# A decoder trunk on one core: the layer norm's variance and root as columns of tokens, sums taken inside the last panel

## The reference

```python
def layer_norm(x, g, b):
    mu = jnp.mean(xf, axis=-1, keepdims=True)
    var = jnp.mean(jnp.square(xf - mu), axis=-1, keepdims=True)
    return ((xf - mu) * lax.rsqrt(var + LN_EPS) * g + b)

for i in range(DEPTH):
    h = layer_norm(DEEPNORM_ALPHA * h + mix, ln1_g[i], ln1_b[i])
    ffn = conv_glu_ffn(h, ffn_w_in[i], ffn_conv_w[i], ffn_conv_b[i], ffn_w_out[i], valid)
    h = layer_norm(DEEPNORM_ALPHA * h + ffn, ln2_g[i], ln2_b[i])
```

## Time and profile before

| | us |
|---|---|
| median of 3 runs | 1401.59 |
| lowest, highest | 1399.56, 1404.59 |
| the profiled execution | 1404.32 |
| its span, first to last instruction | 1402.4 |
| PE busy | 1336.0 (95%) |
| DVE busy | 945.4 (67%) |
| ACT busy | 811.3 (58%) |
| POOL busy | 231.8 (17%) |

### The profile page before, as it was taken

One profiled execution on the slowest core, in us unless ns is written; L12 is line 12 of the kernel. 1 busy time (PEld: TensorE's weight loads), 2 busy tenths in 40 slices (PEclk: granted clock), 3 DMA queues, 4 the chain that ended last, 5 costly groups with the idle time before them and its releaser, 6 DMA issues.

```text
span 1402.4 us, 30127 instructions
## 1 busy us (share of the span) xinstructions
PE 1336.0 (95%) x10433; PEld 1267.9 (90%) x10433; DVE 945.4 (67%) x1890; ACT 811.3 (58%) x1637; POOL 231.8 (17%) x216
## 2 busy tenths in 40 slices
PE   7899999999999999999986999999988999999997
PEld 6788999999977999999975899999987888999997
DVE  4665777765797777765685777776564566777754
ACT  5455676654666666654643567665463555766644
POOL 1000034420000044320010003442000000243400
PEclk9999999999999999999988999999998999999999
DMA  7332455556421456566330135655643333366662
GB/s 256 115 107 74 136 172 187 178 179 195 139 76 49 134 180 188 172 189 188 123 100 31 61 121 170 190 178 180 195 124 119 101 97 122 119 186 190 181 214 86
DMA packets 56867, 203.33 MB, mean 145 GB/s; under 512 B 6224, under 2 KB 8272, under 8 KB 56656
## 3 DMA queue, kind: packets, MB, share of 16 engines
q1 hardware_dynamic: 56784, 202.21, 46.1%
HBM read 201.13 MB, written 1.05 MB: 144 GB/s over the span
## 4 chain that ended last, share of the span: by engine, by line
PE 84%; DVE 7%; ACT 6%; issue 2%; DMA 1%; SPq 0%; DVEq 0%; ACTq 0%
PE ps L376 23%; PE ps L380 22%; PE ps L379 22%; PE ps L494 3%; PE ps L395 2%; PE ps L512 2%; PE ps L398 2%; PE ps L399 2%; DVE w_lo L1135 2%; PE ps L477 1%; PE ps L459 1%; ACT w_hi L765 1%; ACT probs L815 1%; DMA cst<-in_consts 1%; PE ps L577 1%
## 5 line engine op out<-in xcount | busy, mean ns | idle before, releaser
L1135 DVE TENSOR_TENSOR w_lo<-raw,w_hi 128x1024 fp32r<-128x1024 f32 x378 | 462.3, 1224 | 254.3 <-ACT w_hi L765 252.6
L376 PE MATMUL ps<-h_hi,w_hi 128*128 128x272 f32 (+1 forms) x1752 | 511.7, 292 | 7.7 <-DVE q_rope L1325 4.9
L765 ACT ACTIVATE w_hi<-raw 128x1024 fp32r<-128x1024 f32 x378 | 396.8, 1051 | 191.7 <-PE ps L376 180.0
L380 PE MATMUL ps<-h_hi,w_lo 128*128 128x272 f32 (+1 forms) x1752 | 504.8, 288 | 0.0
L379 PE MATMUL ps<-h_lo,w_hi 128*128 128x272 f32 (+1 forms) x1752 | 503.6, 287 | 0.0
L376 PEld LDWEIGHTS ps<-h_hi,w_hi 128*128 128x128 f32 x1752 | 330.8, 189 | 15.7 <-issue 5.9
L379 PEld LDWEIGHTS ps<-h_lo,w_hi 128*128 128x128 f32 x1752 | 331.4, 189 | 0.3
L380 PEld LDWEIGHTS ps<-h_hi,w_lo 128*128 128x128 f32 x1752 | 330.9, 189 | 0.0
L376 PE MATMUL ps<-hid_hi,w_hi 128*128 128x272 f32 (+2 forms) x676 | 198.1, 293 | 0.3 <-DVE y L1135 0.2
L379 PE MATMUL ps<-hid_lo,w_hi 128*128 128x272 f32 (+2 forms) x676 | 195.4, 289 | 0.0
L380 PE MATMUL ps<-hid_hi,w_lo 128*128 128x272 f32 (+2 forms) x676 | 195.4, 289 | 0.0
(11 more groups left out here) (153 smaller groups left out, 1751.2 us busy)
## 6 DMA issues: line engine op xcount, KB each, us to landing
raw<-in_weights SPq DMA_DIRECT2D x378, 512.0 KB, 3.7
cst<-in_consts SPq DMA_DIRECT2D x1, 1795.5 KB, 12.3
h<-in_x SPq DMA_DIRECT2D x2, 544.0 KB, 5.5
out<-h SPq DMA_DIRECT2D x8, 128.0 KB, 1.8
```

The source lines that it names most:

```text
L376: m = pe.matmul(b, whi, xhi, start=n == 0, stop=False)
L380: m = pe.matmul(b, wlo, xhi, start=False, stop=n == len(tiles) - 1)
L765: act.activation(w_hi[slot][:], raw[slot][:], ACT.Copy).then_inc(hi_ready, 1)
L1135: return dve.tensor_tensor(out_, a_, b_, op)
```

## The change

- `totals` gets only chunks 0 to 5 (five additions for each norm in place of six; `add_last` is gone). Chunk 6 and its square go to PE as they are.
- The column sums turn round: the data is the stationary operand (128 channels x 128 tokens) and one column of 1/1024 the moving one, so that a matmul gives one number for each token of a third, down the partitions (`columns`). The thirds are `THIRDS`: tokens 0 to 127, 128 to 255 and 144 to 271. Two matmuls with zeros open the two banks.
- Twelve of the eighteen column matmuls, and the two with zeros, stand inside the last panel, ahead of its last three tiles (`first_sums`, by `inside`). Six stand after the last join and square.
- Square of the mean, variance, square root (ACT's Sqrt, one table load before the last square, none after it) and reciprocal are done on 128 x 3 numbers. The mean and the factor are then spread over the partitions by PE (`spread`: a broadcast column times the identity, three matmuls each), the mean to bank 5, the factor to bank 6, where DVE reads it.
- DVE centers 2 chunks and POOL 6.
- The 28 filling matmuls are now 4, 1, 2 and 8, between the steps.
- A next stage that starts from h uses `leading_from_h`: the two products with `h_hi` wait for `norm_hi` alone, the product with `h_lo` follows for all panels.
- In ACT's program the last unit of `down` is split after the square of chunk 6; DVE splits the last unit of a stage before the last join. After its `h_hi` ACT loads the next table (Silu or Exp) with a dummy operation.

```diff
-CENTER_DVE = 5
+CENTER_DVE = 2
+THIRDS = ((0, P), (P, 2 * P), (T - P, T))
-WARM = 28
-        mean_sq, mean = y[:, 2, :], y[:, 3, :]
+        mean, rstd = y[:, 3, :], ps[:, 6, 0:T]
...
                 for n, (u, t, k) in enumerate(tiles):
+                    if inside is not None and n == len(tiles) - 3:
+                        inside()
...
+            def leading_from_h(n, s, u0, p0, count, t0):
...
+                for k in range(DC - 1):
+                    at_k = slice(k * P, (k + 1) * P)
+                    pe.wait_ge(norm_hi, 8 * n + k + 1)
+                    for j, (b, slot) in enumerate(zip(banks, slots)):
...
+                        m = pe.matmul(b, w_hi[slot][:, at_k], h_hi[:, k, t0:T], start=k == 0, stop=False)
...
+                        pe.matmul(b, w_lo[slot][:, at_k], h_hi[:, k, t0:T], start=False, stop=False)
+                    pe.wait_ge(h_ready, 8 * n + k + 1)
+                    for b, slot in zip(banks, slots):
+                        pe.matmul(b, w_hi[slot][:, at_k], h_lo[:, k, t0:T], start=False, stop=False)
...
-                pe.wait_ge(sums_added, 6 * (n + 1))
-                pe.matmul(ps[:, 5, 0:T], ones, totals[:, 0, :], start=True, stop=False)
-                pe.matmul(ps[:, 6, 0:T], ones, totals[:, 1, :], start=True, stop=False)
+                def columns(b, src, last=False):
+                    for ch, (lo, hi) in enumerate(THIRDS):
+                        ins = pe.matmul(ps[:, b, ch:ch + 1], src[:, lo:hi], ones[:, 0:1],
+                                        start=False, stop=last and ch == 2)
+                    return ins
+                def first_sums():
...
+                    for b in (7, 4):
+                        pe.matmul(ps[:, b, 0:3], zero[:], zero[:, 0:3], start=True, stop=False)
+                    pe.wait_ge(squared, 8 * n + 7)
+                    pe.wait_ge(sums_added, 5 * (n + 1))
+                    for part in (totals[:, 0, :], h[:, 6, :]):
+                        columns(7, part)
+                    for part in (totals[:, 1, :], squares[:, 0, :]):
+                        columns(4, part)
...
+                warm(6, 4)
                 pe.wait_ge(bank_free, p0 + 8)
-                pe.matmul(ps[:, 5, 0:T], ones, h[:, 7, :], start=False, stop=True).then_inc(mean_done, 1)
+                columns(7, h[:, 7, :], last=True).then_inc(mean_col_done, 1)
+                warm(6, 1)
                 pe.wait_ge(squared, 8 * n + 8)
-                pe.matmul(ps[:, 6, 0:T], ones, squares[:, 1, :], start=False, stop=True).then_inc(sq_mean_done, 1)
-                    with pe.Fori(0, WARM // 4):
...
+                columns(4, squares[:, 1, :], last=True).then_inc(sq_mean_done, 1)
+                def spread(b, i):
+                    for ch, c0 in enumerate((0, 0, P - TAIL)):
+                        lo, hi = ch * P, min(T, (ch + 1) * P)
+                        ins = pe.matmul(ps[:, b, lo:hi], col[:, i, ch:ch + 1].broadcast_to([P, P]),
+                                        ident[:, c0:c0 + hi - lo], start=True, stop=True)
+                    return ins
+                pe.wait_ge(mean_col_copied, n + 1)
+                spread(5, 3).then_inc(mean_done, 1)
+                warm(6, 2)
+                pe.wait_ge(rstd_done, n + 1)
+                spread(6, 2).then_inc(rstd_spread, 1)
+                warm(7, 8)
...
-                act.wait_ge(var_done, n + 1)
-                own.link(act.activation(rstd[:], rstd[:], ACT.Ln, bias=eps[:, 0:1]))
-                act.activation(rstd[:], rstd[:], ACT.Exp, scale=-0.5).then_inc(std_done, 1)
...
+                if not last and (n % 2 == 0 or KINDS[(n + 1) // 2] != "mla"):
+                    act.activation(eps[:, 2:3], eps[:, 0:1], ACT.Exp if n % 2 else ACT.Silu)
...
+                    else:
+                        own.link(tt(h[:, k, :], h[:, k, :], ps[:, 5, 0:T], ALU.subtract))
+                    if k == 0:
+                        dve.wait_ge(rstd_spread, n + 1)
-                    dve.scalar_tensor_tensor(h[:, k, :], h[:, k, :], ln_par[:, n, 0, k:k + 1], rstd[:],
+                    dve.scalar_tensor_tensor(h[:, k, :], h[:, k, :], ln_par[:, n, 0, k:k + 1], rstd,
                                              ALU.mult, ALU.mult).then_inc(rescaled, 1)
```

More of the change, by code:

```diff
@@ L180 @@
 CONST, N_CONST = const_columns()
-INITS = 8
+INITS = 9
 def build_program(nc, x, weights, consts, out):
@@ L356, in _, with panel @@
         def _(pe):
-            def panel(s, u0, p0, i, j, rhs, ready, t0):
+            def panel(s, u0, p0, i, j, rhs, ready, t0, inside=None):
                 pn = i * s.body + (p0 + j)
@@ L409, in turn @@
                         if isinstance(i, int) and i == 0 and j < lead:
-                            if j == 0:
+                            if j == 0 and name in ("o", "down"):
                                 leading_panels(s, u0, p0, rhs, ready, lead, t0, range(led, DC))
-                        else:
-                            panel(s, u0, p0, i, j, rhs, ready, t0)
+                            elif j == 0:
+                                leading_from_h(2 * layer + (name == "up"), s, u0, p0, lead, t0)
+                        else:
+                            ending = inside is not None and i == s.turns - 1 and j == s.body - 1
+                            panel(s, u0, p0, i, j, rhs, ready, t0, inside if ending else None)
                         if after is not None:
@@ new lines, in warm @@
+                def warm(b, count):
+                    if n < 2 * DEPTH - 1:
+                        slot = LAYERS[(n + 1) // 2][NEXT[n]][1] % RING
+                        for _ in range(count):
+                            pe.matmul(ps[:, b, 0:T], w_hi[slot][:, 0:P], w_hi[slot][:, P:P + T], start=True, stop=True)
+                gemm(n // 2, stage, rhs, ready, after, lead=lead, straight=True, led=led, inside=first_sums)
+                if n < 2 * DEPTH - 1:
+                    pe.wait_ge(hi_ready, LAYERS[(n + 1) // 2][NEXT[n]][1] + 1)
@@ L782, in turn @@
                     for j in range(s.body):
-                        for u in units_of(layer, name, i, j):
+                        us = list(units_of(layer, name, i, j))
+                        held = us[-1:] if name == "down" and i * s.body + j == DC - 1 else []
+                        for u in us[:len(us) - len(held)]:
                             split_hi(u)
```

79 lines of the change are left out of this document (44 added, 35 removed).

## The result

The changed kernel takes **1432.72 us** (median of 4 runs, 1428.98 to 1436.69) against 1401.38 us for the kernel before in the same comparison (4 runs): a ratio of 1.0209, 95% interval 1.0181 to 1.0237. It is slower by 31.3 us. The profiled execution of the changed kernel took 1428.98 us, with a span of 1427.2 us and a mean granted clock of 0.979 (before: 0.982). That is the fastest of the four, so it shows less than the median loses. The same kernel ran once more beside e1 to e3: one of its four runs took 3318.82 us, over twice the others, and is left out of every number here, so that 1435.65 us, the median of the other three, stands for it.

A forecast was written before the change was run, and what follows sets the result against it. PE bounds the kernel, with 84% of the chain that ended last. Paid 24.6 us for inserted loads, won 8.85 behind the panel: net +15.8, from median 1401.6 to 1417.4 us, range 1403 to 1435.

The forecast's parts named there:

- the price of a load: Inside the last panel: 0.11 us per 128-column load, from the records' slope; 28 loads cost 3.1 us per norm, 24.6 in eight.
- rival 1: In the norms, thin streaming makes the clock fall: 8 to 27 us, most likely 14, so 1431; chance 0.28.
- the 0.9 of `v`: In `v` of layer 3, earlier chunk and buffer against 1.5 us for table and dummy on ACT: 0.9 us won.
- won behind the panel: After the last panel, 8.85 us won: `up` 6.2, `vk` 0.85, `a` 1.2, `v` 0.9, last norm -0.3.
- rival 2: Loads cost 0.08 us each because they overlap the matmuls before them: +4.7 us, 1406.3; chance 0.10.
- Rival 3: Inside the panel, one-column matmuls run nearly free at 0.03 us per load and the kernel gets faster: 1388; chance 0.12.
- rival 4: What is paid inside the panel comes back as less waiting in the next stage: nothing changes, 1401; chance 0.05.
- B': The new end of the last panel, from which the forecast counted times: PE starting at 4.9 us in place of 6.45.
- Its low parts come at 5.1 and then every 0.82, the last at 10.7: DVE's low parts behind the panel: the last at 10.7 us in place of 11.53, 0.85 won where DVE bounds.
- Table load behind `h_hi`: new on ACT after norms 1 and 5, moved ahead after 0, 2, 4, 6: On ACT behind the norms: 1.5 us for table and dummy, counted in `v`, where 0.9 us was still won.
- The row for 41.2 to 44.6: Earlier trace stretch cited for the clock: PE busy 0.93 us of 3.4, clock 0.50 in the next 3.4 us.
- The last norm: Its last product waits for POOL, starting 7.95 us behind the panel in place of 7.7: 0.3 us lost.

The follow-up runs named there:

- e1: Changed kernel with the fourteen matmuls inside the last panel left out, their two waits kept: 1401.03 us, ratio 0.9987 to the kernel before.
- e3: Changed kernel without the table load and dummy operation behind `h_hi`: 1436.93 us, ratio 1.0246 to the kernel before.
- e2: Changed kernel with 128 equal columns streamed in place of one in every column matmul and the zeros' matmuls widened: 1429.97 us, ratio 1.0188.
- e9: e6 with the changed kernel's table load and dummy behind `h_hi` put back: 1404.40 us, ratio 1.0008 to the kernel before.
- e6: Changed kernel, nothing inside the panel, chunk 6 in `totals`, its twelve loads behind the panel streaming 128 columns, no late table load: 1397.18 us, again 1398.53.
- e10: e6 with one column streamed in place of 128 in the twelve matmuls over `totals`: 1405.13 us, ratio 1.0007 to the kernel before.
- e7: Kernel before with fourteen one-column fp32 matmuls, results unused, put inside its last panels: 1433.93 us, ratio 1.0217.
- e5: Kernel before with only the new order of leading panels, PE starting on the high part: 1399.63 us, ratio 0.9964.
- e8: Changed kernel with its fourteen inserted matmuls placed one by one between the long ones of the last panel: 1438.72 us, ratio 1.0259.

## Why the prediction was right, and where it was not

The sign and the range held (1403 to 1435 holds 1432.7), the size didn't: +15.8 was forecast and +31 measured. By the price of a load alone the forecast reached 1428.5 at most; that the range held owes to rival 1, which had widened it. The term missing from the sum is the clock. The terms, each with what the runs give:

| term | forecast, us | measured, us | from |
|---|---|---|---|
| 28 loads inside the panel, 8 norms | +24.6 | +24.3 | 8 x 3.04; e2 with the clock up |
| clock | rival 1 | +10.3 | 34.6 (changed, again, less e1) - 24.3 |
| late table load, with the clock behind its waits | inside the 0.9 of `v` | +5.9 | e9 less e6 |
| all else, won behind the panel | -8.85 | -8.6 | e1's -2.7 less the 5.9 |
| sum | +15.8 | +31.9 | changed, again, less before: 31.9 |

The sum of the measured column is no test of its parts, since the clock's term and the last one are differences; e2 and e10 test the first two by themselves, e9 the third. The -8.6 is the weakest: the 5.9 was measured in e6 and is taken off the time of e1, and single steps of what was to be won came out smaller than forecast (below). Nor is e1's -2.7 a sum of like gains: the stretch of `a` alone is 4.75 us shorter than before and that of `vk` 2.71 longer. That -8.6 lies so near -8.85 may be luck.

- **The price of a load was right.** 3.04 us for 28 is 0.109 each, against 0.11 taken from the slope of the records. What is measured is the load with its one-column matmul; that the load makes the price follows from the slope and isn't tested by itself. The Trainium skill (TensorE: Matmul & The Clock Gate, "Back-to-back issue gap") has about 81 ns for a pair of load and matmul with 128 columns; the trace doesn't agree for these one-column matmuls, and rival 2, which went by it, falls. Rival 3 (0.03) and rival 4 fall with it: e1 and e7 show that what is paid inside the panel doesn't come back.
- **The path behind the panel was nearly right.** With B' = 481.61, as forecast and as measured: columns of chunk 7 end at 1.35 and 1.36, squares 2.13 and 2.16, reciprocal 2.88 and 2.97, mean spread 2.79 and 2.83, factor spread 3.75 and 3.86, first product 3.79 and 3.98, PE 4.9 and 5.09. Each step is a few hundredths late and they add up to 0.19; 1.36 us were won per `up` in place of 1.55. Not all of it is due to the columns: e5 shows that 0.53 came from PE starting on the high part.
- **"Its low parts come at 5.1 and then every 0.82, the last at 10.7" failed.** In the third norm the last stands at 11.31. POOL's six centerings now run beside the low parts and lengthen them. In the kernel before POOL is through at 162.83, ahead of the first low part at 164.15, and the 64 low parts have a mean of 0.49 us. In the changed kernel the 27 that overlap POOL's work have 0.60 and the other 37 have 0.48. The first low part came at 5.27 in place of 5.1, and the first four pitches are 0.93 in place of 0.82: 0.17 and 0.44 make the 0.61 that are missing. In `vk`, where 0.85 was to be won, the last low part stands at B' + 11.30 against 11.59 before: 0.3. I had costed the work on DVE without asking what it now runs beside.
- **"Table load behind `h_hi`: new on ACT after norms 1 and 5, moved ahead after 0, 2, 4, 6" was read too narrowly.** I counted it only in `v`. Moved ahead isn't free: what queues behind it on ACT is the split of the next weight unit, and PE waits for the low part of that. The waits after the change (3.2 and 2.5 us in all, above) were 0.6 and 0.9.
- **Rival 1 wasn't a rival but an addition.** I had set the forecast and the fall of the clock side by side as alternatives and given the forecast the larger chance because PE is occupied throughout. The row for 41.2 to 44.6 was the right precedent: there PE stood idle, here it was occupied and streamed almost nothing, and the clock did the same. Its price was put at 8 to 27 us, most likely 14; 10.3 was measured. With 14 in the forecast it would have read 1431, near the 1432.7 in part by luck: the clock's price was too high and the late table load's 5.9 was missing.
- **The last norm** was to lose 0.3 us to POOL, and this failed. The last join to the end is 12.95 us against 11.41, but the clock fell there in both profiles (from 1413.7 and 1420.8). In e2, whose norms are the same but for the columns and whose clock stayed up until 1431.5, it is 10.96 us. The last product does wait for POOL there, 0.22 us, but starts 7.57 us behind the start of the join, against 7.66 before: POOL's six take 4.35 us, 0.73 each, where no low parts run beside them.

What stays open: why the clock falls at some norms and not at others with the same instructions. The first profile shows it at norms 0, 3, 4, 5 and 7, the second at 0, 1, 3, 4 and 7, so it isn't the program alone that decides.

## What to carry to other kernels

Cost a small matmul by its weights: fourteen fp32 matmuls of one column took as much of PE as 24 long ones, whether in a block or one by one between long ones. Column sums by TensorE paid nothing inside the panel and about 0.15 us per norm behind it, where PE would have stood anyway (5.77 in e6 against 5.92 in e5); there the streams should be kept wide if long matmuls follow. When a dummy table load is moved ahead of a wait, look at what queues behind it on ACT; and where two engines that took turns now overlap, take their durations from a stretch of the trace in which they do.

## What the hardware showed that I had not expected

- **The clock follows what is streamed, not how long PE is occupied.** At 1.00 before and PE busy for all of 3.40 us, the clock still went to 0.50 behind the inserted part (after, e7, e8) and behind the twelve one-column products (e10). With 128 columns in the same places it stayed (e2, e6). It doesn't fall at every such norm. A fall costs 0.4 to 3.2 us behind the panel.
- **More streaming made a kernel faster.** e6 streams 128 columns where e10 streams one, and is 6.6 us faster, clear of the noise. e2 holds PE 0.84 us longer per norm than the changed kernel and is no slower for it; its lead of 5.7 us is within the spread of the runs.
- **POOL and DVE slow each other.** A low part on DVE, which reads `h` and `h_hi`, takes 0.60 us beside POOL's centerings and 0.49 without; a product that reads `h` and the factor in PSUM takes 0.48 to 0.50 in both. Of POOL's six the three beside low parts take 0.97 us each, the three ahead of them 0.77, as much as the three of the kernel before (0.77 to 0.78; the 2.25 us of the earlier trace rows are three that overlap a little). The Trainium skill (SBUF — State Buffer, "Who interferes with whom") says that a DVE instruction with two SBUF inputs contends with a GpSimd one that reads SBUF. The trace agrees on who is slowed. The Trainium skill (same page and section) calls the port pair that the two share "an exclusive lock". What is lost here is far less than the other's whole instruction: 0.11 us for a low part and 0.20 for a centering.
- **A small matmul isn't hidden beside long ones.** In e8 a long matmul and a small one together take 0.35 us, as much as 0.125 and two loads of 0.109 apart.
